# Eight experts in an order computed on the chip, a form for at most 32 tokens, and prefetch hints for the branch into the next expert's form

## What is computed

```python
SEQ, D_MODEL, N_EXPERTS, MOE_TOPK, FFN_EXPERT = 256, 1024, 8, 2, 3584

def _swiglu(h, wg, wu, wd):
    return (jax.nn.silu(h @ wg) * (h @ wu)) @ wd

def _moe(h, router_w, router_b, wg, wu, wd):
    logits = (h @ router_w + router_b).astype(jnp.float32)
    top_v, top_i = lax.top_k(logits, MOE_TOPK)
    top_w = jax.nn.softmax(top_v, axis=-1)
    gates = jnp.sum(top_w[..., None] * jax.nn.one_hot(top_i, N_EXPERTS, dtype=jnp.float32), axis=-2)
    out = jnp.zeros_like(h)
    for e in range(N_EXPERTS):
        out = out + gates[..., e:e + 1] * _swiglu(h, wg[e], wu[e], wd[e])
    return out

for l in range(DEPTH):
    x = x + g1 * _token_mixer(...)
    f = _swiglu(h, ...) if l % 2 == 0 else _moe(h, ...)
    x = x + g2 * f
return _rmsnorm(x, final_norm_w)
```

## Time and profile before

| | us |
|---|---|
| time, median of 3 runs (2046.76 to 2052.06) | 2050.29 |
| the profiled execution: its own time | 2052.97 |
| its span | 2051.2 |
| TensorE busy in the span | 1945.4 |
| first product of expert 0 (start) | 1053.88 |
| end of expert 7's products | 2028.4 |
| mean granted TensorE clock over the span | 0.977 |

### The profile page before, as it was taken

The page is one execution under the profiler, slowest core; times in us unless marked ns, Lnnn a source line. Parts: engine busy times, 40 slices in busy tenths (PEclk is TensorE's granted clock), DMA queues, the critical chain, the costliest instruction groups (busy, mean ns, idle before and its releaser), DMA issues.

```text
span 2051.2 us, 28236 instructions
## 1 busy us (share of the span) xinstructions
PE 1945.4 (95%) x11415; PEld 1379.9 (67%) x11416; DVE 501.9 (24%) x1098; ACT 276.1 (13%) x519; POOL 351.3 (17%) x215
## 2 busy tenths in 40 slices
PE   7999799989999999999979999998988999999998
PEld 5888588867776788888855555554446877554444
DVE  1794734110001391434130101110101100101102
ACT  2104212010001203412020001010000000101002
POOL 2609900079993000000000000000000000000000
PEclk9999899999999999999979999999999999999999
DMA  9746433267773343333479999999999666799840
GB/s 381 256 152 226 164 124 122 85 241 258 269 274 147 121 163 131 117 110 123 174 305 401 420 417 352 417 422 422 422 422 420 241 245 246 308 382 421 311 179 22
DMA packets 73841, 533.82 MB, mean 260 GB/s; under 512 B 8320, under 2 KB 8320, under 8 KB 8960
## 3 DMA queue, kind: packets, MB, share of 16 engines
q1 hardware_dynamic: 67680, 489.72, 60.8%
q0 software_dynamic: 5760, 41.95, 5.6%
q10 hardware_dynamic: 288, 0.50, 0.1%
HBM read 531.08 MB, written 1.05 MB: 259 GB/s over the span
## 4 chain that ended last, share of the span: by engine, by line
PE 84%; SPq 4%; DMA 4%; DVE 4%; ACT 2%; issue 2%; POOL 1%; ACTq 0%; DVEq 0%
PE ps L614 21%; PE ps L953 17%; PE ps L988 9%; PE ps L677 7%; PE ps L686 7%; PE ps L1017 6%; SPq L449 4%; PE ps L697 4%; PE ps L1033 3%; PE ps L912 2%; PE ps L929 2%; DMA ring<-in_moe_units 1%; DMA xc<-in_moe_units 1%; DMA proj<-in_ada_units 1%; PE ps L973 1%
## 5 line engine op out<-in xcount | busy, mean ns | idle before, releaser
L614 PE MATMUL ps<-hT,ring 128*128 128x256 f32 x2048 | 454.4, 383 | 5.0 <-ACT hT L1136 5.0
L614 PEld LDWEIGHTS ps<-hT,ring 128*128 128x128 f32 x2048 | 390.9, 192 | 61.0 <-issue 8.3
L953 PE MATMUL ps<-ring,proj 128*64 128x256 f32 (+2 forms) x1768 | 204.7, 369 | 7.9 <-DMA ring<-in_moe_units 7.9
L534 POOL TENSOR_TENSOR aring<-aring,ccol 128x2048 f32<-128x2048 f32 x40 | 145.0, 3624 | 236.6 <-ACT hT L1136 162.8
L953 PEld LDWEIGHTS ps<-ring,proj 128*64 128x64 f32 (+2 forms) x1768 | 119.6, 134 | 86.1 <-issue 41.0
L1663 DVE TENSOR_TENSOR proj<-proj,ps 128x256 f32<-128x256 f32 (+2 forms) x49 | 23.4, 479 | 616.5 <-PE ps L953 616.5
L686 PE MATMUL ps<-hT,ring 128*128 128x256 f32 x704 | 156.8, 385 | 4.0 <-ACT hT L1136 4.0
L686 PEld LDWEIGHTS ps<-hT,ring 128*128 128x128 f32 x704 | 135.4, 194 | 22.5 <-issue 4.4
L540 POOL TENSOR_TENSOR aring<-aring 128x1024 f32<-128x1024 f32 x80 | 149.4, 1867 | 6.3
L1466 DVE SCALAR_TENSOR_TENSOR misc<-cpad,par,misc 128x256 f32<-128x256 f32 x240 | 102.7, 511 | 0.0
L1259 ACT ACTIVATE proj<-ps 128x256 f32<-128x256 f32 (+2 forms) x49 | 21.0, 429 | 590.6 <-PE ps L953 590.6
(11 more groups left out here) (291 smaller groups left out, 2042.0 us busy)
## 6 DMA issues: line engine op xcount, KB each, us to landing
ring<-in_moe_units SPq DMA_DIRECT2D x144, 1024.0 KB, 14.1
ring<-in_dense_units SPq DMA_DIRECT2D x121, 1024.0 KB, 5.0
aring<-in_moe_units SPq DMA_DIRECT2D x48, 1024.0 KB, 12.7
proj<-in_moe_units SPq DMA_DIRECT2D x48, 1024.0 KB, 16.1
aring<-in_ada_units POOLq DMA_DIRECT2D x40, 1024.0 KB, 6.2
extra<-in_moe_units SPq DMA_DIRECT2D x24, 1024.0 KB, 12.8
xc<-in_moe_units SPq DMA_DIRECT2D x24, 1024.0 KB, 16.3
misc<-in_moe_units SPq DMA_DIRECT2D x24, 1024.0 KB, 18.3
```

What stands on the lines that cost most here:

```text
L534: last = g.tensor_tensor(w, w, ccol[:, :].unsqueeze(2).broadcast_to([P, KT, 256]), ALU.mult)
L614: last = mm(ps[:, n % 2, j * SEQ:(j + 1) * SEQ], wide(s)[:, k, j * P:(j + 1) * P], hT[:, k, :], start=(k == 0), stop=(k == KT - 1))
L953: last = mm(ps[rows * c:rows * (c + 1), bank, 4 * t0:4 * (t0 + rows)], xg[:, 4 * h + k, t0:t0 + rows], w[:, k, 4 * rows * c:4 * rows * (c ...
```

## The change

Six things change.

1. `SIZES` gets a form for at most 32 tokens, `QUARTER`. Its code (`quarter_rows` on TensorE, `part_copy` and `quarter_silu` on ScalarE, `quarter_hidden` on VectorE) runs four products of 32 columns side by side, one for each quarter of the contraction, on 512 columns of weights each. The four partial sums lie in four partition groups; ScalarE copies those of the gate and VectorE those of up out of PSUM, and eight small products with a stacked identity (`sum_and_turn`) add them and transpose at once. Only then come silu (ScalarE, 128 columns) and the multiplication (VectorE, 128 columns).
2. VectorE computes an order of experts 1 to 7 after the router: rank by count, largest first; rank r stands at place min(2r, 13-2r) behind expert 0. It permutes keys, gates and counts into that order (lines 1752 to 1780 of the changed kernel, 24 instructions) and writes the expert numbers to `turn`. With the counts above the order becomes 0, 5, 6, 7, 3, 1, 2, 4, with 24, 153, 20, 128, 30, 67, 41 and 49 tokens; before it was 24, 67, 41, 30, 49, 153, 20 and 128.
3. SP waits for the order (`ord_s`) before the loop and loads two expert numbers from `turn` at the top of each turn; the address of a transfer then uses them.
4. `count_after` waits for `ord_s` too.
5. Right after `count_after`, `toward` branches on the next count and sets a prefetch hint for the branch of the head's chain that leads into that form.
6. The key and gate of expert 0 are made first, alone.

```diff
-SIZES = (HALF, 96, 128, 160, 256)
+SIZES = (QUARTER, HALF, 96, 128, 160, 256)
...
         def count_after(eng, e):
+            eng.wait_ge(ord_s, 1)
             return eng.value_load(cnt[0:1, ds(e + 2, 1)], min_val=0, max_val=SEQ)
...
-                eng.br_cond(count > SIZES[-2], f"{tag}_{SIZES[-1]}", f"{tag}_over_{SIZES[-3]}")
+                to_form[SIZES[-1]] = eng.br_cond(count > SIZES[-2], f"{tag}_{SIZES[-1]}", f"{tag}_over_{SIZES[-3]}")
...
                     ahead = eng.mark_branch_hint_location()
-                    after = expert(n, e, before)
+
+                    def toward(after):
+
+                        def hint(size):
+                            if size in to_form:
+                                to_form[size].branch_hint(eng.mark_branch_hint_location())
+                        by_size(eng, after, hint)
+
+                    after = expert(n, e, before, toward)
...
+            def expert_of(place):
+                return sp.value_load(turn[0:1, place], min_val=0, max_val=EXPERTS - 1)
+
+            sp.wait_ge(ord_s, 1)
             with sp.Fori(0, EXPERTS - 1) as e:
+                now, following = expert_of(ds(e, 1)), expert_of(ds(e + 1, 1))
                 for u in range(EXP_SLOTS, UNITS):
                     sp.wait_ge(unit_s, e * UNITS + (u - EXP_SLOTS + 1))
-                    expert_load(e, u)
+                    expert_load(now, u)
...
+                def quarter_rows(n):
+
+                    def product(kind, g, bank):
+                        for h in range(2):
+                            w = cols4(arrived((kind, g, h)))
+                            for k in range(4):
+                                last = mm(ps[n * k:n * (k + 1), bank, :], xg[:, 4 * h + k, 0:n], w[:, k, :],
+                                          start=(h == 0), stop=(h == 1))
+                            last.then_inc(unit_s, 1)
...
+                    def sum_and_turn(g):
+                        pe.wait_ge(esil_s, S0 + g + 1)
+                        pe.wait_ge(ehm_s, S0 + g + 1)
+                        for part, c0 in ((silx, 0), (hst, P)):
+                            for j in range(4):
+                                last = mm(ps[:, 4 + g % 2, c0 + j * n:c0 + (j + 1) * n],
+                                          part[:, g % 2, j * P:(j + 1) * P], stk[:, :], start=True, stop=True)
+                        last.then_inc(eht_s, 1)
...
+                    for g in range(1, GE):
+                        gate(g)
+                        sum_and_turn(g - 1)
+                        up(g)
+                        if g == 1:
+                            after = count_after(pe, e)
+                            toward(after)
+                            scatter_before()
+                        down_quarter(g - 1)
...
+            then_wait(v.scalar_tensor_tensor(order_c[:, 1, :], order_c[:, 0, :], float(EXPERTS), slot_f[:, 0:EXPERTS],
+                                             ALU.mult, ALU.subtract))
...
+            then_wait(v.tensor_reduce(rank, order_m, AX.X, ALU.add))
+            then_wait(v.tensor_scalar(place, rank, -2.0, 2.0 * OTHERS - 1.0, ALU.mult, ALU.add))
+            then_wait(v.scalar_tensor_tensor(place, rank, 2.0, place, ALU.mult, ALU.min))
...
+            def placed(values, dst):
+
+                then_wait(v.tensor_tensor(order_t, order_m, values.unsqueeze(1).broadcast_to(square), ALU.mult))
+                then_wait(v.tensor_reduce(dst, order_t, AX.X, ALU.add))
...
+            v.tensor_copy(turn[:, :], order_c[0:1, 5, :]).then_inc(ord_s, 1)
+            dve.wait_ge(ord_s, 1)
```

151 lines of the change are left out of this document (135 added, 16 removed).

## The result

The changed kernel takes 2060.6 us (median, 2048.4 to 2067.6) where the kernel before took 2048.4 beside it: a ratio of 1.0047 with an interval of 1.0033 to 1.0061. It is slower by half a per cent where I had forecast 2001 us. Its times also spread wider than those of the kernel before beside it (2046.8 to 2052.6; over the later sets of runs 2043.6 to 2060.6); its profiled execution is a long one, 2067.55 us with a span of 2065.8.

The account below looks back on a forecast made before the run. Full DMA engines and TensorE were taken to bound the kernel in turn. Order some 20, form some 20 and entries 10 us made 50 off 2050.3: forecast 2001 us, chance 0.60, own range 1990 to 2011, range with two rivals 1989 to 2027.

Parts of the forecast that it names:

- The order: Experts' loop: the ring is full before small experts and the last expert has little work left; some 20 us saved.
- The order's calculation: VectorE ahead of its loop: 24 more small steps take 5.0 us, then 2 us until SP issues.
- the 32 form's group: TensorE, 32-token form: three products of 1.8 us plus 1.9 for sum_and_turn make a group of 7.3 us.
- The form's worth: 32-token form in places 0, 2 and 4: it uses up a full ring quickly; some 20 us saved.
- The entry prices in the earlier trace: TensorE's entries: 0.62 us into the 64 form directly behind the comparisons, 3.7 into the 160 and 128 forms.
- the hints do nothing: Rival, entries into forms: early hints fetch nothing, far entries stay and those into 96 and 64 miss; 2018 us, chance 0.18.
- The hints: Entries into places 1 and 3: early hints bring idling of 3.7 us under 1; 10 us saved from the entries.
- The clock in the waits: Rival, 32 form: TensorE's clock falls while waiting, slowing the gather and the next form's start; 22 us, 2023, chance 0.12.
- The other side: Clock stays low through the whole 32 form, 2125 us, slower than before; chance 0.05 together with any other slowing cause.

Follow-up runs that it names:

- the order alone: Changed kernel with the new order but without the 32-token form and without early hints: 2032.9 us, ratio 0.9910 to the kernel before.
- the filler: Changed kernel without early hints, plus 16 unread 32x512 matmuls in four strips in groups 1 to 5 of the 32 form: 2048.5 us against 2047.1 without.
- the tripled sums: Kernel without early hints, 64 form's code first (2052.3 us), with the 32 form's eight small products issued three times in all groups but the last: 2122.0 us.

## Why the prediction was wrong, point by point

- **The order** (20 us): right. 17.7 us; the transfers run on where they idled.
- **The order's calculation** and **the 32 form's group**: right. 4.5 us for the steps against 5.0 forecast, and 2.1 from there to SP's issue against 2; a group of 7.19 us where units lie ready, against 7.3, with sum_and_turn at 1.97, against 1.9. VectorE's timeline (the last step on the gates, the order written), SP's (its fifteenth transfer) and ScalarE's (the copies of two successive groups):

```profile
1053.14 0.17 DVE L1752 COPY gate<-heads 128x2 f32<-128x2 f32 x1
...
1057.68 0.15 DVE L1780 CAST turn<-heads 1x8 int32<-1x8 f32 x1
```

```profile
1059.77 0.96 SPq L467 DMA_DIRECT2D aring<-in_moe_units  x2
```

```profile
1075.75 0.60 ACT L1358 ACTIVATE proj<-ps 128x512 f32<-128x512 f32 x1 [11.33 <-PE ps L1039]
...
1082.94 0.60 ACT L1358 ACTIVATE proj<-ps 128x512 f32<-128x512 f32 x1 [5.04 <-PE ps L1039]
```

- **The form's worth** (20 us): the step that failed. I costed what runs in the 32 form and what runs in the others, from rows of the same size, and carried over places 5 to 7 as 132, 87 and 99. The step took for granted that a form entered without a gap before would be entered so after. Inserting code ahead of it took that away: the gaps grew from 8.8 us with the order alone to 33.8, with slower starts behind them (5.51 to 8.11 us in place 5). The form's own saving of 12 us in places 2 and 4 was less than that. Place 0, given 86 us, took 92.4 to the copy, though its transfers began earlier than I had said: with the order alone it ended at 1144.2, with the form at 1145.2, with the form and the filler at 1142.1, so that some 3 us of the miss are the clock at its end, and the rest stays open.
- **The entry prices in the earlier trace rows**: read rightly, used wrongly. I wrote that the form directly behind the comparisons was entered in 0.62 us and the others in 3.7, and then didn't ask which form would stand there after the change. That single question, put to the 96 and 64 forms in places 5 to 7, gives 3 x 3.7 = 11 us more even by the price then known (the rival "the hints do nothing" had some 7 for it, but no term of the forecast did); measured were 5.6, 6.0 and 9.8, the last because two waits can come in a row.
- **The hints** (10 us): wrong in sign. -13.5 us, with the branches that they stand in. The rival "the hints do nothing" had it right that the far entries stay, with 2018; but it bounded the hints' effect at zero. Right behind the hint stands the scatter, and I didn't cost what the hint might do to the code behind it.
- **The clock in the waits**: the rival's mechanism came (0.50 to 0.58 in single stretches of place 0), its price of 22 us did not show: the filler won 3 us in place 0 and nothing in all. The scatter of place 2 in the changed kernel, at 0.58, is a larger piece (6.5 us longer than at 1.00), and in the 6 us before it the clock stood at 1.00, with TensorE busy for 4.62. The Trainium skill (TensorE: Matmul & The Clock Gate, HAM oscillation) describes the falling clock of a kernel that waits for data between short bursts, and the trace agrees (0.69 from 1100 to 1140, with TensorE busy for 33.04 of 40 us). It fell too while TensorE had no pause, within small matmuls: the tripled sums show that.
- **The other side**: my one mechanism that would end slower was a clock that stays low. The sign came from others, the hints' own cost and the place of the code, for which the rows stood in my own group 5. The range (1989 to 2027) held, but for those 7 us, no case in which the change made a part slower that it didn't touch.

## What to carry over

A kernel with runtime branches between large bodies has a layout: before adding a body, list each transition that the run will take and ask whether its target is next in the code or right behind the comparisons; here each that isn't cost mostly 3.7 to 6 us, and up to twice that when the comparisons had to be fetched as well. Put the bodies that follow one another most often there, or leave a form out: in this kernel the 64 form used for everything up to 64 tokens beats the better-fitting 32 form by 14 us. A hint for a branch isn't free: behind these stood gaps of up to 1.7 us in the code that followed; measure it alone.

## What the runs showed of the hardware

- Code that is never executed made a kernel 51 us slower (2032.9 to 2083.8), by its place alone; moving one body to the end made it 38 us slower, with 20 more fetches of 16.4 kB (96 to 116).
- A taken branch to far code idled TensorE for 3.7 us out of the 64 form standing first and mostly for 5 to 6 otherwise (2.4 to 3.3 in three entries), and mostly 8 to 12 when the comparisons had to be fetched too. Within such a gap of 10.64 us the instruction queue moved a block of 16 kB, and two more 6 us later. A hint for the back branch took 3 to 4 us off (9.66 to 6.00, 3.70 to 0.78); hints for the branches behind it took off 0.9 at most.
- TensorE's clock fell from 2.4 to 1.2 GHz with the engine busy 14.00 of 14.00 us, within series of matmuls of 128 x 32. With 16 wide matmuls and 8 small ones in a group, in place of 24 small ones, it stayed at 1.00.
- 32 records of 32 x 512 took 13.90 us when all wrote the same 32 partitions, and 3.62 when they went to four strips in turn.
